# Hybrid attention block: attention begins after three projections, the other projections run as planned pieces inside it

## What is computed

```python
h = rms_norm(x, norm1)
dq, dk, dv, nq, kc, vc, ksl, vsl, kw, vw, gt = split(h @ w_in)   # 1024 -> 2840 columns
o_diff = 4 heads: softmax(q1 k1 + bias) - lam * softmax(q2 k2 + bias), times v (128 wide), rms_norm
kc_c, vc_c = gelu(blocks(kc) @ w1) @ w2, the same for vc         # 31 blocks of 32 positions, hidden 256
o_nsa = g0 * compressed attention + g1 * selected attention + g2 * window attention   # 8 heads, 64 wide
x = x + concat(o_diff, rms_norm(o_nsa)) @ w_out
x = x + (silu(h2 @ w_gate) * (h2 @ w_up)) @ w_down               # hidden 2816, h2 = rms_norm(x, norm2)
out = rms_norm(x, final_norm)
```

## Time and profile before

| what | value |
|---|---|
| time, three executions | 743.21, 744.69, 746.9 us, median 744.69 |
| profiled execution, first to last instruction | 740.7 us |
| TensorE busy | 695.3 us, 94% |
| VectorE busy | 339.0 us |
| ScalarE busy | 278.3 us |
| GpSimd busy | 248.4 us |
| mean granted TensorE clock | 0.969 |
| cast to w_hi, L748 | 96 times, mean 1050 ns |
| split to w_lo, L420 | 96 times, mean 2438 ns |

### The profile page before, as it was taken

One profiled execution on the slowest core, in us unless ns is written; L12 is line 12 of the kernel. 1 busy time (PEld: TensorE's weight loads), 2 busy tenths in 40 slices (PEclk: granted clock), 3 DMA queues, 4 the chain that ended last, 5 costly groups with the idle time before them and its releaser, 6 DMA issues.

```text
span 740.7 us, 9658 instructions
## 1 busy us (share of the span) xinstructions
PE 695.3 (94%) x3541; PEld 581.9 (79%) x3541; DVE 339.0 (46%) x819; ACT 278.3 (38%) x546; POOL 248.4 (34%) x121
## 2 busy tenths in 40 slices
PE   5998989999897997997999999999999999999995
PEld 4885678997797996786878888888888888888884
DVE  6521377577667778774436334334334321003004
ACT  4401565565454545552454323223223222114112
POOL 6601521031211211023317443544544434434422
PEclk7999999999999998999999999999999999999998
DMA  7447532031121111012315333323233233233202
GB/s 235 82 143 234 163 93 65 8 93 36 36 65 36 39 57 35 2 58 66 87 47 163 93 87 112 87 87 112 86 90 109 86 95 104 86 104 96 86 1 114
DMA packets 84227, 64.42 MB, mean 87 GB/s; under 512 B 2424, under 2 KB 75204, under 8 KB 84180
## 3 DMA queue, kind: packets, MB, share of 16 engines
q1 hardware_dynamic: 80160, 58.83, 26.9%
q10 hardware_dynamic: 3444, 4.48, 1.9%
q0 software_dynamic: 576, 0.49, 0.6%
HBM read 61.67 MB, written 4.47 MB: 89 GB/s over the span
## 4 chain that ended last, share of the span: by engine, by line
PE 84%; DVE 7%; DMA 4%; issue 3%; ACT 2%; SPq 0%; POOL 0%; DVEq 0%; ACTq 0%
PE bank L462 14%; PE bank L464 14%; PE bank L463 14%; PE bank L444 9%; PE bank L445 9%; PE bank L446 9%; PE bank L608 5%; DMA raw<-in_w_in_dram 4%; PE bank L585 3%; PE bank L569 2%; PE bank L570 2%; PE bank L456 2%; PE bank L519 1%; DVE bank L1054 1%; DVE k_diff L1035 1%
## 5 line engine op out<-in xcount | busy, mean ns | idle before, releaser
L420 POOL TENSOR_TENSOR w_lo<-raw,w_hi 128x1024 fp32r<-128x1024 f32 (+1 forms) x96 | 233.7, 2438 | 468.8 <-ACT w_hi L748 468.8
L748 ACT CAST w_hi<-raw 128x1024 fp32r<-128x1024 f32 (+1 forms) x96 | 100.4, 1050 | 275.3 <-PE bank L464 143.9
L462 PE MATMUL bank<-xT_hi,w_hi 128*128 128x512 f32 x480 | 191.9, 400 | 1.8 <-POOL w_lo L420 1.5
L464 PE MATMUL bank<-xT_hi,w_lo 128*128 128x512 f32 x480 | 190.0, 396 | 0.0
L463 PE MATMUL bank<-xT_lo,w_hi 128*128 128x512 f32 x480 | 189.6, 395 | 0.0
L462 PEld LDWEIGHTS bank<-xT_hi,w_hi 128*128 128x128 f32 x480 | 90.9, 189 | 21.7 <-POOL w_lo L420 2.0
L464 PEld LDWEIGHTS bank<-xT_hi,w_lo 128*128 128x128 f32 x480 | 91.0, 189 | 20.6
L463 PEld LDWEIGHTS bank<-xT_lo,w_hi 128*128 128x128 f32 x480 | 91.0, 190 | 18.2 <-issue 0.2
L816 ACT ACTIVATE E<-bank,nmax 128x128 f32<-128x128 f32 (+3 forms) x96 | 50.8, 529 | 76.3 <-DVE nmax L1054 76.2
L446 PE MATMUL bank<-w_hi,act_lo 128*128 128x512 f32 x176 | 69.0, 392 | 0.0
L444 PE MATMUL bank<-w_hi,act_hi 128*128 128x512 f32 x176 | 69.0, 392 | 0.0
(11 more groups left out here) (175 smaller groups left out, 934.2 us busy)
## 6 DMA issues: line engine op xcount, KB each, us to landing
raw<-in_w_gate_dram SPq DMA_DIRECT2D x22, 512.0 KB, 3.9
raw<-in_w_up_dram SPq DMA_DIRECT2D x22, 512.0 KB, 3.9
raw<-in_w_down_dram SPq DMA_DIRECT2D x22, 512.0 KB, 3.8
raw<-in_w_in_dram SPq DMA_DIRECT2D x20, 512.0 KB, 3.9
raw<-in_w_out_dram SPq DMA_DIRECT2D x8, 512.0 KB, 3.8
bias_rows<-bias_scratch ACTq DMA_DIRECT2D x1, 2304.0 KB
xres<-in_x_dram SPq DMA_DIRECT2D x4, 512.0 KB, 5.3
raw<-in_cmp_w_k_dram SPq DMA_DIRECT2D x4, 512.0 KB, 4.4
```

The lines of the kernel that those rows point to most:

```text
L420: nc.gpsimd.tensor_tensor(wv_lo(k)[:, 0:n], raw[:, raw_of[("chunk", k)] % RAW_SLOTS, 0:n], wv_hi(k)[:, 0:n].bitcast(F32), ALU.subtract).th ...
L462: nc.tensor.matmul(bank[:, :], hi, xT_hi[:, kt, :], start=kt == 0, stop=False)
L464: return nc.tensor.matmul(bank[:, :], lo, xT_hi[:, kt, :], start=False, stop=kt == KT - 1)
L748: nc.scalar.copy(wv_hi(k)[:, 0:n], raw[:, raw_of[("chunk", k)] % RAW_SLOTS, 0:n]).then_inc(s_whi, 1)
```

## The change

- The projections become jobs (`PROJ_JOBS`). Before attention run q0, ksl and the two vg jobs (`BASE_JOBS`), then kw as a lead; c0, c1, the hidden layers (`h`), their turn (`ht`) and end (`hc`), and all others are pieces inside attention. The turns of the nsa half of mix (`mt`) and W_out's lower half (`og`) are jobs of the same list.
- The pieces of a slot come from a plan by prices: `slot_us` for what a slot costs TensorE, `PIECE_US` for a piece (0.69 otherwise); the planner levels price per slot against due times three slots ahead, and a job begins no sooner than one slot after the one two before it.
- A job that ends in slot s is evacuated by ScalarE and VectorE in slot s+1. VectorE gathers slot s-5 in place of s-4. For k, ScalarE writes hi to both halves and VectorE subtracts twice from PSUM; the copies L1036 and L1037 go.
- w1 has a buffer of its own of four slots of 256 KB, loaded in 16 parts by SyncE. It and `blk` lie where xres lies, so x is loaded a second time after the hidden layers.
- The start: three small loads move from GpSimd's queue to ScalarE's, the bias vector and the bias rows are made earlier and sent by SyncE between chunk 2 and chunk 3, x tiles are turned as they come with filler matmuls between them, and the first cast to w_hi comes after the last root.
- The last two down chunks run block by block (`last_rows`), and the end of each block is done at once.

```diff
-WARM = 16
+WARM = 12
+WARM_GAP = (7, 5, 2, 8)
+W1_SLOTS = 4
-PIECES = 8
-PIECES_PER_SLOT = 1.35
-LEAD_PIECES = 6
-FILL_RATE = 2.5
+LEAD_JOBS = 1
+AHEAD = 3
+PROJ_JOBS = [("q", 0), ("k", "ksl"), ("vg", 0), ("vg", 1), ("k", "kw"),
+             ("q", 1), ("c", 0), ("dq", 0), ("dk", 0), ("dv", (0, 0)), ("dv", (0, 1)), ("q", 2), ("c", 1),
+             ("h", 0), ("h", 1), ("dq", 1), ("dk", 1), ("ht", 0), ("q", 3), ("hc", 0),
+             ("dq", 2), ("dk", 2), ("dv", (1, 0)), ("dv", (1, 1)), ("dq", 3), ("dk", 3)]
+BASE_JOBS = 4
+PIECES = {"ht": 1, "hc": 1, "mt": 1, "og": 4}
+PIECE_US = {"h": 0.86, "ht": 0.45, "hc": 0.9, "mt": 0.45, "dv": 0.73}
...
+def slot_us(slot):
+
+    kind, _, b, i = slot
+    if kind == "cmp":
+        return 2.9
+    us = (0.23, 0.24, 0.35, 0.46)[i]
+    return us if kind == "diff" and b == 0 else us + 0.336 * (i + 1)
...
     for s in range(n_slots + 4):
+        rate = max((sum(cost[done:upto]) + sum(own[s:d + 1])) / (d + 1 - s) for d, upto in due if d >= s)
+        lag = min(lag + rate - own[s], 4.0)
+        must = needed(slots[s + AHEAD]) if s + AHEAD < n_slots else 0
+        while done < len(pieces):
+            j, p = pieces[done]
+            if s < first_slot.get(jobs[j][0], 0) or (j >= must and lag < cost[done] / 2 and s < n_slots + 3):
+                break
+            if p == 0 and any(ended[z] >= s for z in after(j)):
+                break
+            lag -= cost[done]
+            done += 1
+            ended[j] = s
+        piece_upto.append(done)
...
+            for k in range(len(chunks)):
+                if k == RAW_SLOTS:
+
+                    sp.wait_ge(s_bvec, 1)
+                    sp.dma_start(bias_scratch[:, :], bias_vec[:, :]).then_inc(s_scratch, 16)
+                    sp.wait_ge(s_scratch, 16)
+                    sp.dma_start(bias_rows[:, :, :], bias_scratch[:, :].unsqueeze(1).to_broadcast([NHEADS, P, 384])).then_inc(s_spread, 16)
+                if k >= RAW_SLOTS:
+                    sp.wait_ge(s_split, k - RAW_SLOTS + 1)
...
+                if chunks[k] == ("c", 1):
+                    load_w1(0, W1_SLOTS)
+                if chunks[k] == ("dq", 2):
+                    load_w1(W1_SLOTS, 16)
+                if chunks[k] == ("dv", (1, 1)):
+
+                    sp.wait_ge(s_job, job_of[("h", 1)] + 1)
+                    for t in range(NT):
+                        sp.dma_start(xres[:, t, :], x[0, t * P:(t + 1) * P, :]).then_inc(s_x[t], 16)
...
+            for t in range(NT - 1):
+                pe.wait_ge(s_norm, t + 1)
+                turn_x(t, range(6))
+                keep_warm(WARM_GAP[t])
...
+                if kind == "h" and a == 1:
+
+                    act.wait_ge(s_evac, j + 1)
+                    nc.scalar.activation(hid_rows[:, :, :], hid_rows[:, :, :], ACT.Gelu_apprx_tanh).then_inc(s_gelu, 1)
...
+                        nc.scalar.activation(k_[0:HD, :], src, ACT.Copy).then_inc(s_hi, 1)
+                        nc.scalar.activation(k_[HD:P, :], src, ACT.Copy).then_inc(s_hi, 1)
...
-                            link(nc.vector.tensor_tensor(lo[0:HD, :], src, hi[0:HD, :].bitcast(F32), ALU.subtract))
-                            nc.vector.tensor_copy(hi[HD:P, :], hi[0:HD, :])
-                            ins = nc.vector.tensor_copy(lo[HD:P, :], lo[0:HD, :])
+                            dve.wait_ge(s_hi, hi_before[j] + 2 * hd + 2)
+                            for half in range(2):
+                                ins = nc.vector.tensor_tensor(lo[half * HD:(half + 1) * HD, :], src,
+                                                              hi[half * HD:(half + 1) * HD, :].bitcast(F32), ALU.subtract)
...
-                if s >= 4:
-                    gather(s - 4)
+                if s >= 5:
+                    gather(s - 5)
...
+            def last_rows(k, banks):
+
+                pe.wait_ge(s_split, k + 2)
+                for t in range(NT):
+                    for kw in (k, k + 1):
+                        for kk in range(2):
...
+                    mm.then_inc(s_last, 1)
...
             for t in range(NT):
                 dve.wait_ge(s_last, t + 1)
                 add_residual(t, 1, FOUR[0])
+                if t == NT - 1:
+                    final_scale(t - 1)
+                final_mean(t)
+                final_inverse(t)
+                if t < NT - 2:
+                    final_scale(t)
```

More of the change, by code:

```diff
@@ new lines, in hymba_block, with after @@
+    first_slot = {"mt": cmp_last + 6, "og": cmp_last + 7}
+    def after(j):
+        kind, a = jobs[j]
+        return [j - 2] + {"h": [job_of.get(("c", a))], "ht": [job_of[("h", 1)]], "hc": [job_of[("ht", 0)]],
+                          "og": [job_of[("mt", NT - 1)]]}.get(kind, [])
+    ended = {j: -1 for j in range(BASE_JOBS)}
+    piece_upto, done, lag = [], 0, 0.0
+    while jobs[pieces[done][0]] != jobs[BASE_JOBS + LEAD_JOBS]:
+        ended[pieces[done][0]] = -1
+        done += 1
+    lead = done
@@ new lines, in hymba_block @@
+    own = [slot_us(x_) for x_ in slots] + [1.0] * 4
+    cost = [PIECE_US.get(jobs[j][0], 0.69) for j, _ in pieces]
+    due = [(s, sum(1 for j, _ in pieces if j < needed(slots[s + AHEAD]))) for s in range(n_slots - AHEAD)]
+    due.append((n_slots + 3, len(pieces)))
+    for s in range(n_slots + 4):
+        rate = max((sum(cost[done:upto]) + sum(own[s:d + 1])) / (d + 1 - s) for d, upto in due if d >= s)
[8 more added lines that the diff above has]
+            lag -= cost[done]
+            done += 1
+            ended[j] = s
+        piece_upto.append(done)
@@ L457, in turn_tile, with keep_warm @@
                 mm.then_inc(s_tp, 1)
+            def keep_warm(n):
+                for _ in range(n):
+                    nc.tensor.matmul(ps[0][:, 3 * P:4 * P], ones[:, :], ones[:, :], start=True, stop=True)
             def columns(bank, k, kt):
@@ L642, in _ @@
+            pe.wait_ge(s_norm, NT)
+            turn_x(NT - 1, range(KT))
+            for j in range(BASE_JOBS):
+                if j == 1:
+                    pe.wait_ge(s_tlo, KT)
+                proj_job(j)
+            upto = 0
+            while upto < lead:
+                proj_piece(*pieces[upto])
                 upto += 1
```

685 lines of the change are left out of this document (310 added, 375 removed).

## The result

| kernel | median us | lowest to highest | profiled span |
|---|---|---|---|
| before | 745.8 | 743.21 to 747.41 | 740.7 |
| changed | 760.62 | 759.59 to 762.04 | 757.8 |

The ratio is 1.0194, with a 95% interval of 1.0165 to 1.0223. The forecast was 711.3, the range 701 to 724, and slower had a chance of 0.03. It missed by 49.3 us.

What follows compares the result with a forecast made beforehand. TensorE was busy 695.3 of 740.7 us, with VectorE deciding where its holes are. Turn of the last mix tiles 31.5 us earlier and last tile 1.9 gave 707.3; plus 4.0 for the median, 711.3, range 701 to 724.

Steps and rivals of the forecast that it cites:

- second v/g chunk beside bias_rows: Before slot 0: its weight lands near 27, just in time behind the bias_rows transfer; 1 us of stall, 8 if late.
- evacuation one slot late: In attention: the k evacuations fit on ScalarE and VectorE alone and come one slot later; cost 0.
- new form of the k evacuation: In diff(2): k copies go (3.2 us), 1.4 of new subtractions come; reading PSUM, it cannot be caught by a split.
- diff(2): Slots 84 to 91, with dk3, three cmp gathers and four mixT splits: 22.3 us against 18.1 planned, 4 us of stalls.
- GpSimd's lock: GpSimd and certain VectorE instructions lock each other out for a whole instruction; two locks of 1.5 us counted in diff(1).
- slow clock: In attention: 2 us for clock drops somewhere, besides the 3 us of diff(1) that include its slow clock.
- last tile: End of the kernel: the last residual starts at once and the end comes at 735.0; gain 1.9 us.
- Rival C: Start: the first weights are late behind bias_rows, 6 to 8 us more, 718; chance 0.07.
- Rival D: Attention: the lock opens a hole at nearly every job, 68 us more, 779, slower than before; chance 0.03.
- Rival B: Diff stretches: VectorE becomes the bound and each hole halves the clock, 26 us of stalls, 723; chance 0.13.
- diff(1): Diff head in attention with q3, dq2 and the compression's end: VectorE 21 against TensorE's 19.3, 3 us with slow clock.
- GELU: Between exponentials in attention: two table loads at 1.28 plus 0.55 delay ScalarE by 3.1; with dk1, 2 us of stalls.

Runs made afterwards that it cites:

- f1_warm: Changed kernel with 30 small matmuls ahead of the first turn of the NSA half of mix and 16 ahead of the first output group: 759.22 us.
- f3_all_cap: Changed kernel with start in order, own-slot evacuation, splits in quarters, last root ahead of two casts, and planner's cap 2.0 in place of 4.0: 727.07 us.
- e7_same_hold: Changed kernel with evacuation in the job's own slot, and the last six pieces of dk3 spread over slots 85 to 89: 751.08 us.
- e4_same_slot: Changed kernel with finished jobs, except output groups, evacuated in the slot in which TensorE ends them: 748.22 us.
- e8_same_quarters: Changed kernel with evacuation in the job's own slot, and each GpSimd split made in four instructions: 738.54 us.
- five edits: Start in order, own-slot evacuation, splits in quarters, last root ahead of two casts, planner's cap 2.0, all on the changed kernel: 727.07 us.
- the mended one: Changed kernel with four edits: start in order, own-slot evacuation, splits in quarters, last root ahead of two casts; old cap: 731.85 us.
- e9_same_mt: Changed kernel with evacuation in the own slot only for dk3 and the four turns of the NSA half of mix: 748.29 us.

## Why the prediction was wrong

| part | booked | shown by runs |
|---|---|---|
| second v/g chunk beside bias_rows | 1 | 10.3, with what stood behind it on ScalarE |
| evacuation one slot late | 0 | 12.4, all of it with dk3 and the mix turns |
| new form of the k evacuation | -1.8, in diff(2) only | gains 6.4 |
| GpSimd's lock | in the stalls | 9.7; 12.4 in the kernel before |
| the planner's cap | 0 | 4.8 with the other edits, none seen without |
| slow clock | 2, and a part of 3 | about 4 in the stretch from slot 84 to slot 92 alone (trace of f1_warm) |
| last tile | -1.9 | -1.9 |

**The sum was never held against the time that TensorE has to lose.** This is the step that failed first. I forecast the turn of the last mix tiles 31.5 us earlier with the same matmuls. Before that turn TensorE stood idle for 36.8 us in all, so at the same busy time the forecast left 5.3 us of idle time, while my own list had 11 us of stalls, 2 at the turn and a start that TensorE spends partly waiting. Busy time can shrink as well, where the clock rises, but hardly enough: it is 304.2 us up to the turn in the kernel before, and 301.1 in the best run of the new plan (f3_all_cap). The two could not both be true.

The profiled execution missed the 707.3 us by 50.5: 8.3 before slot 0, 40.4 from slot 0 to the turn, 1.8 behind it. From slot 0 to slot 84 the code's prices add up to 201.7 us and it took 218.2, of which TensorE stood 16.5. From slot 84 to the turn they add up to 45.9; with what I booked for diff(2), for the slots behind it and for the turn that is about 56, and it took 81.6. The kernel before took 60.2 us for these slots with eight projection pieces fewer in them, so the terms for diff(2) and for the slots behind it were furthest off. A hidden gain stood in the prices: I took 6 us off because two short samples of the earlier trace rows ran 2.5% below them on average, and because I held the tail steps for too dear. The changed kernel took 49.3 us from slot 64 to slot 84 by prices of 49.4, and 30.6 from slot 32 to slot 44 by prices of 28.1, where the h pieces are. The prices were right or too cheap there. TensorE was busy 260.1 us from slot 0 to the turn, where I had 241.6; a part of this is the clock, since 58.4 of these us stand behind slot 84 at 0.84, and e7_same_hold did the same 282 matmuls in 53.0 at 0.97. Two slips of the working are small beside this: 2.5% of 247.6 and 1.5 make 7.7 and not 6, and 25 less 3.2 plus 1.4 is 23.2 and not 22.3. Slot 0 being 32 us earlier says nothing: the work that stood before it stands inside now.

**Start.** "The weight lands near 27, just in time" failed (34.8). I worked out the length of the spread alone as 9 us and let it end near 25; it was issued at 14.70 and moved beside other loads. Rival C had the mechanism and nearly the price (8), with a chance of 0.07. What I did not see is that mending it by SyncE's order alone gives less than half (4.1 us), because ScalarE's wait for the spread has the next jobs behind it.

**Evacuations.** "Alone they fit, and they are one slot later: 0" failed; this one sentence cost 12.4 us. I counted the busy time of the edit, and not who waits behind it: in slot 88 the bias, the exponentials and the gathering stand behind the subtractions, and TensorE has no pieces then. For diff(2) I took 22.3 us from slot 84 to slot 92; it took 41.4 (25.3 in the kernel before), and from slot 92 to the turn 40.2.

**Form of the k evacuation.** My reason for it (it reads PSUM and cannot be caught by a split) was right, and its worth was mis-sized: 6.4 us where I booked 3.2 less 1.4 in one stretch and nothing elsewhere.

**Lock.** Products of 1.7 us were seen as said, and scores waited for exponentials less than the 13 us of the earlier trace rows. Rival D, which made the lock the danger of this change, had the wrong cause. Rival B was nearer than its 723 us: VectorE did bound a diff stretch, and a granted clock of 0.61 followed from 300 to 320 us, but the order of the evacuation was worth 10.4 us in the stretch from slot 84 to the turn (e4_same_slot), and the shorter splits 2.0 on top (e8_same_quarters). That it costs both kernels 10 to 12 us was open to me in the earlier trace rows.

**Clock.** I booked 2 us for it, and some in the 3 of diff(1). It fell to 0.61 from 300 to 320 us. The low clock is a consequence of the waits, and it has a price of its own: I estimate 4 us there, 1.7 and 2.2 from the trace of f1_warm. How much of the 49.3 us is clock in all was not measured.

**GELU.** Its table loads took 1.28 us each, with the next instruction 1.30 after the start of the load (173.09 and 174.39), and no wait of TensorE over 0.25 us stands between 112 and 186 us, so its 2 us were too many. The estimate by the 2.66 us of the Trainium skill (page "ScalarE: Activation LUTs", section "What ACT_TABLE_LOAD costs") was rightly left out: the trace does not show the drain that this figure holds.

**Root at the end.** "No split runs then" failed: two splits run from 352.35 to 357.21, beside the four scalings (353.60, 4.56 us). TensorE waited 4.3 us for the scalings, 2.85 with splits in quarters and 1.3 with the root ahead of the casts; I had booked 2 us of idle time.

**Last tile.** Right: from the start of the last matmul to the end 9.5 us before (731.23 to 740.7), 7.5 after (750.27 to 757.8). The last stage is still as long as before, in part since the first 16.04 us behind the turn became 17.16, at a clock of 0.85 in place of 0.92.

What stays open: with all mended the time is 727, not 711, and the stretch from slot 84 to the turn still takes 64.7 us, where I had about 56. The five edits sum to 38.7 us by their single prices while the kernel is 33.5 us faster than the changed one. How much of this is overlap, and how much the spread of the runs, was not told apart.

Is the change worth it? With quarters in both, the kernel before has 733.8 and the mended one 731.9, with intervals that overlap. So the change as a whole, mended, brings nothing measurable with the old cap; with the smaller cap it has 727.1. What its parts (the early slot 0, the plan by prices, the later gathering) bring one by one was not tested.

## What to carry to other kernels

Before adding up what a new order of the same work will save, add up the idle time of the engine that bounds the kernel, stage by stage: the saving can be larger only by what a higher clock takes off the busy time, and each stall you expect must still fit in what is left. When a run shortens a stretch, look at idle time and busy time apart: in f3_all_cap the same matmuls became faster and the idle time stayed. Before you call filler harmless or useless, look in the trace whether it stands inside the wait. When an evacuation is moved by one step, look for the step in which the bounding engine has no other work, and follow there, engine by engine, what is queued behind it. Cut long GpSimd instructions that run beside VectorE into parts: it gave 1.7% in a kernel of hand-tuned order.

## What the runs showed of the hardware

- A split in four instructions costs GpSimd 3.1 us in place of 2.4 (1024 columns; 285.5 us for all 96 splits in place of 233.5), and still makes both kernels 10 to 12 us faster.
- A load of 0.5 MB issued 4.75 us behind one of 2.3 MB landed 15 us after its issue (19.45 to 34.8); the load of the same chunk without it was cast, and its split done, in time for the job to wait 0.9 us.
- Small matmuls in a wait of 7.1 us, and more behind a wait of 3.1, raised the mean granted clock of the stretch from 0.75 to 0.92. The same 18 matmuls took 6.39 us at 0.63 and 4.22 at 1.00.
- Waits differ in worth: 5.4 us at slot 54 stayed in e9_same_mt, which reached the whole gain of e4_same_slot, and one of 7.0 us stands in the fastest kernel.
